# The mixer's output projection in seven partial products, its sums added to the residual one by one

## What is computed

```python
def mixer_block(u, cos, sin, w_in, conv_w, q_norm_g, k_norm_g, w_conv_out, w_attn_out, w_o):
    ...
    y_conv = (cb * z) @ w_conv_out
    ...
    y_attn = bidirectional_gqa(q, k, v) @ w_attn_out
    merged = jax.nn.sigmoid(gc) * y_conv + jax.nn.sigmoid(ga) * y_attn
    return merged @ w_o

def hier_moe(u, w_group, w_router, w1, w3, w2):
    grp_logits = (hf @ w_group).astype(jnp.float32)
    ...
    g = jnp.argmax(grp_logits, axis=-1)
    ...
    top_v, top_i = lax.top_k(sel, TOP_K)
```

## Time and profile before

| | us |
|---|---|
| median of 3 runs | 1951.5 |
| lowest, highest | 1950.1, 1953.34 |
| profiled execution | 1948.61 |
| its span | 1946.9 |
| its mean granted TensorE clock | 0.918 |
| TensorE busy in the span | 1583.3 (81%) |
| VectorE busy | 690.6 (35%) |
| ScalarE busy | 302.3 (16%) |

### The profile page before, as it was taken

One profiled execution on the slowest core, in us unless ns is written; L12 is line 12 of the kernel. 1 busy time (PEld: TensorE's weight loads), 2 busy tenths in 40 slices (PEclk: granted clock), 3 DMA queues, 4 the chain that ended last, 5 costly groups with the idle time before them and its releaser, 6 DMA issues.

```text
span 1946.9 us, 22318 instructions
## 1 busy us (share of the span) xinstructions
PE 1583.3 (81%) x9722; PEld 963.2 (49%) x9722; DVE 690.6 (35%) x1451; ACT 302.3 (16%) x804; POOL 12.6 (1%) x37
## 2 busy tenths in 40 slices
PE   9999999999999999775655665655656465999999
PEld 7675567755699995222221222212222112457886
DVE  2673455634486864212110111111111101145533
ACT  0243313433122102000000000000000000223220
POOL 0000000000000000000000000000000000000000
PEclk9999999999999999988787888778888778999999
DMA  9751276414243456999999999999999999944200
GB/s 377 270 147 52 88 290 217 130 44 165 102 163 141 174 217 263 428 432 432 430 430 431 430 430 432 430 427 431 425 423 430 433 430 428 341 151 176 97 32 22
DMA packets 87787, 554.48 MB, mean 285 GB/s; under 512 B 4512, under 2 KB 11424, under 8 KB 74112
## 3 DMA queue, kind: packets, MB, share of 16 engines
q1 hardware_dynamic: 86544, 548.81, 70.1%
q0 software_dynamic: 1136, 4.10, 0.6%
HBM read 551.85 MB, written 1.05 MB: 284 GB/s over the span
## 4 chain that ended last, share of the span: by engine, by line
PE 59%; DMA 35%; DVE 4%; ACT 1%; issue 0%; SPq 0%; POOL 0%; DVEq 0%; ACTq 0%; POOLq 0%
PE bank L676 27%; DMA ring<-in_w 22%; DMA arena<-in_w 13%; PE bank L1153 8%; PE bank L703 6%; PE bank L685 6%; PE bank L1181 3%; PE bank L664 2%; PE bank L1471 1%; PE bank L874 1%; PE bank L808 1%; PE bank L788 1%; DMA prm<-in_pk 1%; DVE arena L2123 0%; PE bank L1424 0%
## 5 line engine op out<-in xcount | busy, mean ns | idle before, releaser
L1153 PE MATMUL bank<-ring,arena 128*32 128x512 f32 x1216 | 285.6, 729 | 153.7 <-DMA arena<-in_w 101.0
L676 PE MATMUL bank<-arena,ring 128*128 128x128 f32 (+1 forms) x2528 | 393.6, 315 | 0.5 <-DVE arena L3081 0.5
L676 PEld LDWEIGHTS bank<-arena,ring 128*128 128x128 f32 x2528 | 357.1, 191 | 28.0 <-issue 4.3
L1153 PE MATMUL bank<-arena 128*32 128x512 f32 x832 | 228.4, 720 | 104.7 <-DMA ring<-in_w 104.7
L1153 PEld LDWEIGHTS bank<-ring,arena 128*32 128x32 f32 x1216 | 71.3, 131 | 276.3 <-issue 276.3
L676 PE MATMUL bank<-ring,arena 128*128 128x512 f32 (+3 forms) x520 | 205.2, 544 | 1.7 <-DVE ring L2418 0.8
L1153 PEld LDWEIGHTS bank<-arena 128*32 128x32 f32 x832 | 55.8, 129 | 189.2 <-issue 189.0
L1181 PE MATMUL bank<-ring,arena 128*32 128x512 f32 x576 | 118.0, 645 | 25.7 <-DMA arena<-in_w 17.1
L676 PEld LDWEIGHTS bank<-ring,arena 128*128 128x128 f32 x520 | 96.1, 190 | 84.1 <-issue 72.3
L703 PE MATMUL bank<-ring,arena 128*128 128x512 f32 (+1 forms) x320 | 129.2, 561 | 2.2 <-DMA ring<-in_w_vd 1.0
L685 PE MATMUL bank<-arena,ring 128*64 128x256 f32 x1024 | 112.7, 380 | 0.0
(11 more groups left out here) (403 smaller groups left out, 1513.9 us busy)
## 6 DMA issues: line engine op xcount, KB each, us to landing
ring<-in_w SPq DMA_DIRECT2D x53, 4096.0 KB, 31.6
arena<-in_w SPq DMA_DIRECT2D x35, 4096.0 KB, 38.0
ring<-in_w_in SPq DMA_DIRECT2D x40, 2048.0 KB, 8.2
ring<-in_w_mod SPq DMA_DIRECT2D x6, 2048.0 KB, 12.4
ring<-in_w_out SPq DMA_DIRECT2D x6, 2048.0 KB, 7.9
arena<-in_w SPq DMA_DIRECT2D x6, 2048.0 KB, 10.5
ring<-in_w SPq DMA_DIRECT2D x6, 2048.0 KB, 12.1
ring<-in_w_out SPq DMA_DIRECT2D x16, 512.0 KB, 9.0
```

The costliest lines, as they stand in the source:

```text
L676: i = te.matmul(ps, lhsT, rhs, start=n0 + k == 0, stop=n0 + k == n - 1)
L1153: m = te.matmul(ps[32 * j:32 * j + 32, :], LM.xg[:, f, 128 * k + 32 * j:128 * k + 32 * j + 32], vs[j][:, 512 * (k % 2):512 * (k % 2) + 512 ...
```

## The change

`w_o` becomes the eighth member of the chain of seven-part products. `mixer_order` and the attention stay as they are.

- VectorE forms the weight sums of `wo2` within the steps of `ya` (the fourth behind them), and four token sums of `mg` behind `ya`'s last part. Here the token sums lie in `late_sums`, three of which move by 256 floats.
- TensorE takes tokens as the stationary operand (results have tokens on partitions, as `h` has) and forms seven parts of four 512-wide matmuls each, in banks `P[k % 4]`.
- VectorE adds partial sums to `h` as they become known; ScalarE copies part 1 to `s1`. The last pieces become final in the order (0,0), (0,1), (1,1), (1,0).
- TensorE's and ScalarE's orders of turns, logits and rank follow that. `root` waits for both pieces.
- SP issues units 6, 7, 2, 8, 9, 3 in place of 2, 3, 6, 7, 8, 9, with two more waits.

The diff, cut to its core:

```diff
-            late_sums = [ar(o, 4, 128) for o in (18448, 23312, 23824, 24336)]
+            late_sums = [ar(o, 4, 128) for o in (18448, 23056, 23568, 24080)]
...
-            for u, name in ((2, ("T", 0)), (3, ("T", 1)), (6, ("ya", 0)), (7, ("ya", 1)), (8, ("wo2", 0)), (9, ("wo2", 1))):
+            for u, name in ((6, ("ya", 0)), (7, ("ya", 1)), (2, ("T", 0)), (8, ("wo2", 0)), (9, ("wo2", 1)), (3, ("T", 1))):
+                if u == 8:
+                    s.wait_ge(*at.of("used", ("wo2", 0), "sums"))
+                if u == 3:
+                    s.wait_ge(*at.of("h", 2, 1, 0))
                 ring_unit(u, name)
...
-                for k in range(2):
-                    t.also("used", ("T", k))
...
             def mixer_out():
+                w0, w1, sums = weights(("wo2", 0)), weights(("wo2", 1)), L2.late_sums
+                first, second = slice(0, 128), slice(128, 256)
+
+                def wo2(k, xT, w, lo=0, hi=4):
+                    ps = P[k % 4]
                     if lo == 0:
+                        fresh("P", "wo2", k, b=k % 4)
+                    i = product(ps[:, :], [(xT[:, c, :], w[:, c, :]) for c in range(lo, hi)], lo, 4)
+                    if hi == 4:
+                        i.then_inc(*t.done("mm", "P", "wo2", k))
                 def turn_h(tt, g):
                     t.wait_ge(*at.of("h", 2, tt, g))
                     turn(("h2T", tt, g), [(128 * i, h[:, tt, 512 * g + 128 * i:512 * g + 128 * i + 128]) for i in range(4)],
                          b=4 + 2 * tt + g)
+                def logits(tt, g, n0):
                     ps = P[tt]
+                    if n0 == 0:
                         fresh("lg", tt, b=tt)
                         t.wait_ge(*at.of("router"))
                     t.wait_ge(*at.of("ev", "h2T", tt, g))
                     i = product(ps[:, 0:72], [(LM.u2[:, c, tt * 128:tt * 128 + 128], wr[:, c, :])
+                                              for c in range(4 * g, 4 * g + 4)], n0, 8)
+                    if n0:
                         i.then_inc(*t.done("mm", "lg", tt))
+                ready(("sum", "ya", 11), ("sum", "ya", 12), ("w", ("wo2", 0)))
+                wo2(1, L2.mg[:, 0:4, first], w0[:, 0:4, :])
+                wo2(2, L2.mg[:, 4:8, first], w0[:, 4:8, :])
+                t.also("used", ("wo2", 0))
+                ready(("T", "wo2", 2), ("S", 3))
+                wo2(3, sums[1], L2.t2)
                 turn_h(0, 0)
+                wo2(4, sums[0], L2.t1)
+                t.also("used", ("T", 0))
+                wo2(5, sums[3], w1[:, 4:8, :])
+                ready(("T", "wo2", 3))
+                wo2(6, sums[2], w1[:, 0:4, :], 0, 2)
                 turn_h(0, 1)
+                wo2(6, sums[2], w1[:, 0:4, :], 2, 4)
+                t.also("used", ("wo2", 1))
+                logits(0, 0, 0)
+                logits(0, 1, 4)
+                ready(("T", "wo2", 4))
+                wo2(7, L2.mg[:, 4:8, second], L2.t4, 0, 2)
+                turn_h(1, 1)
+                wo2(7, L2.mg[:, 4:8, second], L2.t4, 2, 4)
+                t.also("used", ("T", 1))
+                t.also("mixer", "PE")
+                logits(1, 1, 0)
+                rank(0)
                 turn_h(1, 0)
+                logits(1, 0, 4)
                 rank(1)
                 steady(0)
...
-                    ready(("h", 2, tt, 1))
+                    ready(("h", 2, tt, 0), ("h", 2, tt, 1))
...
                                   scale=LM.rstd[:, tt:tt + 1]).then_inc(*a.done("u", tt))
+                ready(("mm", "P", "wo2", 1), ("sum", "ya", 11))
+                se.copy(L2.s1, heads(bank("P", "wo2", 1)[:, :], 128)).then_inc(*a.done("ev", "P", "wo2", 1))
                 h_turned(0, 0)
+                h_turned(0, 1)
                 root(0)
-                h_turned(0, 1)
                 normed(0)
+                h_turned(1, 1)
                 h_turned(1, 0)
-                h_turned(1, 1)
                 root(1)
                 normed(1)
                 pg, e1 = LM.rb[:, 88:90], LM.rb[:, 82:84]
...
-                n = SEVEN.index(name)
+                n = (*SEVEN, "wo2").index(name)
-                    new = SEVEN[n + 1] if n + 1 < len(SEVEN) else None
+                    new = (*SEVEN, "wo2")[n + 1]
...
                     part_sum(name, 11, 2, L2.s1)
                     to_sum(L2.y1, name, 4, L2.s2)
-                    if new:
-                        weight_sum(new, 1)
+                    weight_sum(new, 1)
                     to_sum(L2.s3, name, 5, L2.s2)
                     part_sum(name, 22, 4, L2.s3, L2.s2)
                     part_sum(name, 12, 6, L2.y1)
-                    if new:
-                        weight_sum(new, 2)
+                    weight_sum(new, 2)
                     part_sum(name, 21, 7, L2.s3)
                     if name == "cb":
...
-                    if new:
-                        weight_sum(new, 3)
+                    if name == "ya":
+                        behind()
+                        token_sums(3, L2.mg, L2.late_sums)
+                    weight_sum(new, 3)
...
+                weight_sum("wo2", 4)
...
-                def summed(tt, g):
+                s1, s2, y1 = (ap.rearrange("p a b -> p (a b)") for ap in (L2.s1, L2.s2, L2.y1))
+                def ps(k):
+                    v.wait_ge(*at.of("mm", "P", "wo2", k))
+                    return bank("P", "wo2", k)[:, :]
+                def added(tt, g, src):
                     hv = h[:, tt, 512 * g:512 * g + 512]
-                    v.wait_ge(*at.of("mm", "wo2", tt, g))
-                    ve.scalar_tensor_tensor(hv, bank("wo2", tt, g)[:, :], 0.5, hv, ALU.mult, ALU.add
-                                            ).then_inc(*v.done("ev", "wo2", tt, g))
-                    v.also("h", 2, tt, g)
+                    behind()
+                    return ve.scalar_tensor_tensor(hv, src, 0.5, hv, ALU.mult, ALU.add)
+                def token_rows(tt, g, src, k):
+                    added(tt, g, src).then_inc(*v.done("h", 2, tt, g))
+                    v.also("ev", "P", "wo2", k)
...
-                summed(0, 0)
-                summed(0, 1)
+                ready(("ev", "P", "wo2", 1))
+                added(0, 0, s1).then_inc(*v.step())
+                token_rows(0, 0, ps(2), 2)
+                ve.tensor_tensor(s2, ps(3), s1, ALU.add).then_inc(*v.done("ev", "P", "wo2", 3))
+                behind()
+                ve.tensor_tensor(y1, ps(4), s2, ALU.add).then_inc(*v.done("ev", "P", "wo2", 4))
+                added(0, 1, y1).then_inc(*v.step())
+                token_rows(0, 1, ps(5), 5)
+                added(1, 1, y1).then_inc(*v.step())
+                added(1, 0, s2).then_inc(*v.step())
+                added(1, 1, ps(6)).then_inc(*v.done("h", 2, 1, 1))
+                added(1, 0, ps(6)).then_inc(*v.done("ev", "P", "wo2", 6))
                 scales(0)
                 group(0)
-                summed(1, 0)
+                token_rows(1, 0, ps(7), 7)
                 two(0)
-                summed(1, 1)
                 places(0)
                 group(1)
                 scales(1)
```

More of the change, by code:

```diff
@@ L1021, in mixer_out @@
             def mixer_out():
-                def wo2(tt, g, lo, hi):
-                    ps = P[2 * tt + g]
+                w0, w1, sums = weights(("wo2", 0)), weights(("wo2", 1)), L2.late_sums
+                first, second = slice(0, 128), slice(128, 256)
+                def wo2(k, xT, w, lo=0, hi=4):
+                    ps = P[k % 4]
                     if lo == 0:
[L1026 to L1032, removed]
+                        fresh("P", "wo2", k, b=k % 4)
+                    i = product(ps[:, :], [(xT[:, c, :], w[:, c, :]) for c in range(lo, hi)], lo, 4)
+                    if hi == 4:
+                        i.then_inc(*t.done("mm", "P", "wo2", k))
                 def turn_h(tt, g):
@@ L1037, in turn_h @@
                          b=4 + 2 * tt + g)
-                def logits(tt, g):
+                def logits(tt, g, n0):
                     ps = P[tt]
-                    if g == 0:
+                    if n0 == 0:
                         fresh("lg", tt, b=tt)
@@ L1045, in logits @@
                     i = product(ps[:, 0:72], [(LM.u2[:, c, tt * 128:tt * 128 + 128], wr[:, c, :])
-                                              for c in range(4 * g, 4 * g + 4)], 4 * g, 8)
-                    if g:
+                                              for c in range(4 * g, 4 * g + 4)], n0, 8)
+                    if n0:
                         i.then_inc(*t.done("mm", "lg", tt))
-                ready(("sum", "ya", 11), ("sum", "ya", 12))
-                wo2(0, 0, 0, 8)
-                wo2(0, 1, 0, 4)
-                turn_h(0, 0)
-                wo2(0, 1, 4, 8)
-                ready(("sum", "ya", 21), ("sum", "ya", 22))
-                wo2(1, 0, 0, 2)
-                turn_h(0, 1)
[L1057 to L1061, removed]
-                turn_h(1, 0)
[L1063 to L1068, removed]
```

(10 more changed lines are left out.)

## The result

| | before | after |
|---|---|---|
| median of 12 runs, us | 1949.37 | 1953.53 |
| lowest to highest | 1946.93 to 1953.34 | 1950.68 to 1957.42 |
| profiled span | 1946.9 | 1955.7 |

The ratio is 1.0021, 95% interval 1.0014 to 1.0029: 4.1 us slower (2.7 to 5.6), against 1.6 forecast. The kernel before now has a median 2.1 us lower than the one that stood over the prediction (more runs), so the difference is what to compare, not the level. That the new median, 1953.53, lies close to the forecast level, 1953.1, is luck.

A forecast was written before the change was run, and what follows sets the result against it. The experts' DMA weight stream was taken as fixed behind the first use of unit 0. TensorE's -1.2 and the tail's +2.8 gave +1.6 on 1951.5, so 1953.1, with a range of 1947.5 to 1957.5.

The forecast's parts named there:

- The frame: Experts' weight stream: time is first use of unit 0 plus a fixed stream; unit 10's issue moves from 776.55 to 778.2.
- The DMA reordering: Units 2, 3 and 6 to 9 issued in new order; unit 3, the late one, in by 772, cost taken as nothing.
- The landing of `w_o`: First weight sum on VectorE waits until the second half lands at 723.4, holding VectorE 2.8.
- The byte count: Rival, chance 0.22: by bytes moved `w_o` is in at 721.0, so no change, 1951.5.
- The two stalls: TensorE idle 2.4 ahead of the turn of h(0,0) and about 2.3 at `rank(0)`, each waiting on VectorE.
- the tail: From the last product to group 1: routing of token half 0 now in series, 6.2 in all, +2.8 in the sum.
- TensorE's own gain of 1.2: Up to the last product's end: 3.5 by four fewer products, 0.5 by earlier start, less 2.4 and 0.2 of waits.
- the clock's term: TensorE stall of 2.4 inside dense products: effect on the clock not shown, lower end nothing, added as nothing.
- The rival's price, 3.4: Clock rival, chance 0.18: both new stalls bring TensorE's clock down, +3.4 on top of +1.6, 1956.5.
- the signs of being wrong: First issue moves but span doesn't, first issue comes before 776, or the clock falls in the stage.
- the weights in time: Rival, chance 0.22: `w_o` wait ends at 721.0, TensorE stands 1.2, group 1 at 765.7; no change, 1951.5.
- the whole saving: Rival, chance 0.10: four products fewer on TensorE and nothing late, -3.5, 1948.0.

The follow-up runs named there:

- e2: Changed kernel with both halves of `w_o` issued ahead of expert units 0 and 1; ratio 1.0011 against the kernel before, +2.1 us.
- e3: Changed kernel with `two(0)` ahead of part 7's addition and the last turn of h ahead of `rank(0)`; ratio 1.0005 against the kernel before, +1.0 us.
- e5: Changed kernel with the third and fourth weight sums moved behind the first two additions to h; ratio 1.0008 against the kernel before, +1.6 us.
- e4: Changed kernel with the edits of e2, e3 and e5 together; ratio 0.9989 against the kernel before, -2.1 us.
- e1: Changed kernel with four filler matmuls, two ahead of the turn of h(0,0) and two ahead of `rank(0)`; ratio 1.0011 against the kernel before, +2.1 us.
- e7: Kernel before, without the change, with seven VectorE operations added ahead of its first addition to h; ratio 1.0017 against the kernel before, +3.3 us.
- e6: e4 with one filler matmul behind `logits(1, 1, 0)`; ratio 0.9978 against the kernel before, -4.3 us.

## Why the prediction was right or wrong

**The frame was right.** The change is worth what it does to the first issue behind the gap in the stream; the kernels of the table agree within their intervals, all but the changed one, which is 0.2 us outside, and the rest of the span didn't follow the kernel. The direction was right, the size was not: 1.6 forecast, 2.7 to 5.6 measured, while the forecast put 0.74 on a change too small to tell. The DMA reordering in front of it had no price: unit 3 was issued at 765.20 and no wait for it is seen.

**The landing of `w_o` was right**: 723.4 forecast, 723.2 measured in old time. The byte count, 721.0, was the rival and is out. It overlooked a fifth load: in the trace before, unit 5 was issued at 708.04, and the rate stays at 436 to 438 GB/s from 721 to 725, so the 8.40 MB moved by 721 needn't be those of the four first loads. What I weighed from the Trainium skill (DMA: Bandwidth & Descriptors, Queues, rings and completion order) is no date either: it gives the order in the ring and says that completion doesn't follow it. `e2` shows that this wait and its share of the stall can be taken away.

**The two stalls were right** in place, cause and length (2.4 and 2.3 forecast, 2.29 and 2.08 measured), and so was the reading that TensorE's 3.5 are given back by them and by the tail. `e3` and `e5` take each stall away by itself, `e4` both. TensorE's own gain of 1.2 was right too, though the terms named for it (3.5, 0.5, 2.4 and 0.2) give 1.4: by `e1` the last product ends 1.25 earlier than before. The tail was slightly too dear: in `e1` `group(1)` starts 1.3 later than before (1.6 forecast). Behind it the kernel before waits 0.43 for POOL ahead of its gather and `e1` doesn't, which the prediction didn't see, so the order of work costs the stage only 0.9.

**The step that failed is the clock's term.** "What is not shown: a TensorE stall of 2.4 inside dense products, for the clock" was taken at nothing in the sum, with 0.18 for the rival. It measured 4.9 in the stage, by `e1`: 1.8 for the first fall and 3.1 for the second. The rival's price, 3.4, took the 1.7 of the earlier trace rows for each. That was right for the first; the second fall lasted twice as long, over work that lies on the chain. Its time, 1956.5, or +5.0, lay nearer to +4.1 than my +1.6. The clock's fall in the stage was also among the signs of being wrong that the prediction named, and it came; the first issue came at 782.3 in old time, against 778.2 forecast and 781.6 with the rival's 3.4. The Trainium skill (TensorE: Matmul & The Clock Gate, HAM oscillation), cited there as a warning, was right in kind for this kernel. Its rule is for longer gaps than the 2.29, 2.08 and 0.61 behind which the clock fell here, and the measurement decides; `e7` shows that it isn't a matter of a gap's length alone.

**Of the rivals**, the weights in time and the whole saving are out: VectorE did wait, and the stage grew. The whole saving exists, but only with another order: `e6` has 3.8 of stage, near the 3.5 of four products.

## What to carry to other kernels

Fewer products save only where the engine that prepares and adds them isn't put in front of its own consumer: count what is queued ahead of the first addition, and put work that is due later behind it. A wait for a load that nobody waited for before has to be dated from its landing, not its bytes, and is cured by issuing it ahead of loads due much later. Ahead of a DMA-bound stretch read the issue that restarts the stream; and price a new TensorE stall of 2 us at its length, with half-rate work behind it as the upper end (1.8 and 3.1 here, nothing in `e7`); a filler matmul in the stall is the cheap test.

## What was not expected of the hardware

- The granted clock fell to 0.50 behind a TensorE stall of 0.61 us in a stretch of small matmuls in both executions of `e4`, and didn't in the one of `e3`, which has a stall of the same length at the same place; behind 2.29 it fell in all three executions of the changed kernel, behind 2.31 in neither of `e7`'s, behind 1.58 not in `e2`.
- The start of the stage differs by 1.5 us between executions of one program (unit 4 at 671.63 and 673.12 in the two of `e4`), so single spans say little of a change of 2 us; distances inside the trace do.
